# Loads of the next stage issued before both changes of stage, and the attention's product of outputs and gates moved from VectorE to POOL

## Chip, cores and metric

One core of a Trainium2 chip runs the whole program. The metric is the time of one execution in microseconds on the device. Three runs of the kernel before gave 4301.88, 4308.98 and 4311.59 us; the median is 4308.98.

## What is computed

One layer of a hybrid decoder on 2048 tokens and 16 learned meta tokens ahead of them, 1024 channels, float32. The input is RMS-normalised and projected; one branch is an RWKV-7 recurrence, the other stick-breaking attention. Each is multiplied by its own gates, projected, merged, projected again, normalised and added to the input. The change touches the attention branch and what lies on its two sides. Cut to what matters:

```python
q, k, v = heads of the projection, 16 heads of 64 channels
z = q @ k.T * 64 ** -0.5
log_keep = where(visible, log_sigmoid(-z), 0)
log_between = reverse_cumsum(log_keep) - log_keep
weights = where(visible, exp(log_sigmoid(z) + log_between), 0)
y_attention = (weights @ v) * silu(g)
```

The kernel gets `weights @ v` in another way: a reversed running product of `sigmoid(-z)` along the keys (`kept`) gives what is left of the stick, and its transpose is multiplied with the differences of neighbouring values (`dv`).

## The kernel before

`program` (L2132) runs four stages; between them stand barriers of all engines, and everything that passes from one stage to the next goes through scratch tensors in HBM.

1. **Projection**, `project_phase` (L61), called for half A and half B of the tokens. A loop over eight pairs of heads; TensorE multiplies ten blocks of weights in each (L338 to L340), the other engines make from the products what the later stages read. SyncE loads weights (L182) and stores results. In the loop POOL makes the gains, keys and steps (L824 to L844); VectorE has the running sums (a scan, L664) and splits weights into a high and a low part (a cast, L794, and a difference, L647). Semaphores of the stage are cleared by `release` (L2140) after half B, with a barrier (L2143).

2. **Attention**, `attention_phase` (L954). The work is ordered by a list that `attention_schedule` writes out. A group `g` is four tiles of 128 queries of one head; each head has four groups, and the list has 64. In a pair of heads the groups' ranks are 0, 1, 2, 3 for the even head and 3, 2, 1, 0 for the odd one; a group of rank r sees 4(r+1) tiles of keys, so the groups at the middle of a pair are the largest. For each piece of up to 512 keys TensorE makes logits in two passes (L1134 with k_high, L1135 with k_low), ScalarE takes the sigmoid (L1202), VectorE scans it backwards (L1237 for the first piece of a row, with the mask `hidden` as second input; L1240 for the others). For each tile of keys TensorE transposes `kept` (L1145), ScalarE copies that to `w` (L1212), and TensorE adds its products to `acc` (L1172), even and odd tiles of keys in separate halves of the partitions. TensorE interleaves the logits of the next group with the transposes and products of this one, and its products lag three steps behind its transposes.

   At the end of a group ScalarE copies acc's lower half (L1217), VectorE adds the halves to `total` (L1246) and multiplies that with the gates to `y` (L1250). This "sum" comes in ScalarE's and VectorE's lists four steps of values into the next group. SyncE waits for each y (`y_done`), stores it (L1072), loads the gates of group g + 2 (L1068), and then what `due_after(g)` lists: after the groups 0, 1 and 2 of a pair k_high, k_low with the steps `dv`, and `dv_diag` of the odd head, after 3, 4 and 5 queries with k_high, k_low with the steps, and dv_diag of the next even head, after 7 the queries of the next odd one. For head 0 the loads come in three parts (`FIRST_PARTS`) at the stage's start.

   POOL clears two rows of dv and the eight w (L1255, L1257) and then has one duty: as soon as dv_diag of a head has landed it loads the last partition of it, the edges (L1261, from `scr_v_edge`). TensorE waits for dv's steps and for the edges before the first product of a head (`value_steps`).

3. **RWKV**, `rwkv_programs` (L1277), a pipeline over 33 chunks of 64 tokens; SyncE first loads four constants and the first chunk's keys (KB), queries (AR) and values (VU), and TensorE begins with transposes of KB (L1421).

4. **Branches and output**, in the same block as stage 3. Nothing of them is changed.

Of the kernel before, what the change touches and what calls it, by code (L numbers as in the profile page):

```python
# [13 lines left out]
P = 128  # L14
D = 1024
# [45 lines left out]
def project_phase(nc, sem, t, io, scratch, half):  # L61
# [21 lines left out]
    with ExitStack() as ctx:  # L83
# [4 lines left out]
        up, cols = sb("up", [P, P]), sb("cols", [P, N_COLS])  # L88
        raw = [sb(f"raw{x}", [P, 1 + N]) for x in "rkv"]
        mix = [sb(f"mix{x}", [P, N]) for x in "rkv"]  # L90
        difs = [sb(f"dif{b}", [P, max(size for _, size in SG)]) for b in range(3)]
        lora = sb("lora", [P, N])
        run, rate = sb("run", [P, N]), sb("rate", [P, N])
        keep, grow = sb("keep", [P, NCG, CHUNK + 1]), sb("grow", [P, NCG, CHUNK])
        unit, gain = sb("unit", [P, N]), sb("gain", [P, N])
        ar, kb = sb("ar", [P, NCG, 2, CHUNK]), sb("kb", [P, NCG, 2, CHUNK])
# [721 lines left out]
        def _(pool):  # L818
# [34 lines left out]
            with pool.Fori(0, PAIRS) as k:  # L853
# [4 lines left out]
                for g, (at, size) in enumerate(SG):  # L858
                    value_steps(k, g, at, size)

# [6 lines left out]
def keys_of(qt):  # L867

    return META + P * (qt + 1)
# [84 lines left out]
def attention_phase(nc, sem, t, io, scratch):  # L954
# [5 lines left out]
    LAG, ZB, TB, KB, WB = 3, 2, 4, 4, 8  # L960
    FIRST_PARTS = [(0, GROUP), (GROUP, 2 * GROUP), (2 * GROUP, QT)]
    last_logits = {e[1]: e[5] for e in order if e[0] == "logits"}
    last_values = {e[1]: e[3] for e in order if e[0] == "values"}
    with ExitStack() as ctx:
        sb = lambda name, shape, dt=F32: ctx.enter_context(nc.sbuf_tensor(name, shape, dt))
        ps = lambda name, shape: ctx.enter_context(nc.psum_tensor(name, shape, F32))
        q_parts = [sb(f"q_parts{b}", [P, SEQ], F32R) for b in range(2)]
        k_high = [sb(f"k_high{b}", [P, META + SEQ], F32R) for b in range(2)]
        k_low = [sb(f"k_low{b}", [P, META + SEQ], F32R) for b in range(2)]
        dv = [sb(f"dv{b}", [P, 1 + QT, DH]) for b in range(2)]  # L970
        dv_diag = [sb(f"dv_diag{b}", [P, QT, DH]) for b in range(2)]
        longest = sum(keys_of(qt) for qt in range(QT - GROUP, QT))
        shortest = sum(keys_of(qt) for qt in range(GROUP))
        kept = [sb(f"kept{b}", [P, shortest if b >= 2 else longest]) for b in range(4)]
        keep = [sb(f"keep{b}", [P, 512]) for b in range(KB)]
        w = [sb(f"w{b}", [P, 512]) for b in range(WB)]
        low_half = sb("low_half", [DH, 512])
        total = sb("total", [DH, 512])
        gate = [sb(f"gate{b}", [DH, 512]) for b in range(2)]
        y = [sb(f"y_sb{b}", [DH, 512]) for b in range(2)]  # L980
        hidden = sb("hidden", [P, 512])
# [4 lines left out]
        const_in, cleared = sem("a_const_in"), sem("a_cleared")  # L986
        qk_first, v_first = [[sem(f"a_{x}_first{b}") for b in range(len(FIRST_PARTS))] for x in ("qk", "v")]
        edge_first, edge_in = [sem(f"a_edge_first{b}") for b in range(len(FIRST_PARTS))], [sem(f"a_edge_in{b}") for b in range(2)]
        diag_first, diag_in = [sem(f"a_diag_first{b}") for b in range(len(FIRST_PARTS))], [sem(f"a_diag_in{b}") for b in range(2)]
# [5 lines left out]
        y_sent = [sem(f"a_y_sent{b}") for b in range(2)]  # L995
# [44 lines left out]
        def _(sp):  # L1040
            def load_queries(head, first, last, done):
                u, rows, qs = head % 2, slice(DH * head, DH * head + DH), slice(P * first, P * last)
                sp.dma_start(q_parts[u][0:DH, qs].bitcast(F32), scratch["q_hi"][rows, qs]).then_inc(done, 16)
                sp.dma_start(q_parts[u][DH:P, qs].bitcast(F32), scratch["q_lo"][rows, qs]).then_inc(done, 16)

            def load_keys(head, first, last, dst, name, done):
# [3 lines left out]
                for part in (slice(0, DH), slice(DH, P)):  # L1050
                    sp.dma_start(dst[u][part, ks].bitcast(F32), scratch[name][rows, src]).then_inc(done, 16)
# [1221 lines left out]
```

## Time and profile before

| | |
|---|---|
| median of 3 runs | 4308.98 us (4301.88 to 4311.59) |
| profiled execution | 4298.37 us |
| its span, first to last instruction | 4296.6 us |
| TensorE busy | 4141.8 us (96%) |
| VectorE busy | 2380.7 us (55%) |
| ScalarE busy | 1663.7 us (39%) |
| POOL busy | 813.6 us (19%) |
| projection | up to about 2025 us |
| attention | about 2025 to 3026 us |
| mean granted clock of TensorE | 0.988 |

Engines are named PE (TensorE), PEld (its weight loads), DVE (VectorE), ACT (ScalarE), POOL and SP (SyncE; SPq is its queue). Times in the views are microseconds from the start of the span. "L1246" is a line of the kernel. In a timeline a row has its start, how long it took, engine, line, operation, out<-in, how many like it were merged into it, and in brackets how long the engine had stood idle and what ended that. A DMA's own time in a timeline is that of its issue. Ends of matmuls are modelled.

### The profile page before, as it was taken

How to read it: one execution, taken by the hardware profiler on the slowest of the kernel's cores; microseconds unless marked ns; L12 is line 12 of the kernel's file. 1: busy time of each engine (PE TensorE's matmuls, PEld its weight loads, DVE VectorE, ACT ScalarE, POOL GpSimd, SP SyncE). 2: the span in 40 equal slices, each digit the busy share in tenths (PEclk: the TensorE clock that was granted, in tenths of full speed). 3: DMA queues.
4: the chain of work that ended last, by engine and by line, in shares of the span. 5: the costliest groups of instructions: out<-in, count | busy, mean ns of one | idle time of the engine just before them, and what ended most of it. 6: DMA issues, size and time to landing. Idle time of an engine off the chain costs nothing. (4 is left out here: it accounts for less than half of the span.)

```text
span 4296.6 us, 90884 instructions
## 1 busy us (share of the span) xinstructions
PE 4141.8 (96%) x35784; PEld 3330.3 (78%) x35784; DVE 2380.7 (55%) x3103; ACT 1663.7 (39%) x3296; POOL 813.6 (19%) x655
## 2 busy tenths in 40 slices
PE   7999999997999999998999999999799999999999
PEld 7888899986788888886666666666688888878887
DVE  5344454443444444444888877778567677633222
ACT  4222222223222222222667666766344444421112
POOL 3101111112111111110000000000356666600222
PEclk9999999998999999999999999999999999999999
DMA  2333333334334333334433443442333333365553
GB/s 91 115 120 120 112 111 103 110 101 138 99 103 118 105 106 110 111 117 138 101 83 77 99 92 82 87 85 58 98 111 101 101 101 101 87 202 175 185 187 125
DMA packets 487561, 479.81 MB, mean 112 GB/s; under 512 B 261200, under 2 KB 371408, under 8 KB 481504
## 3 DMA queue, kind: packets, MB, share of 16 engines
q1 hardware_dynamic: 475168, 450.33, 37.5%
q10 hardware_dynamic: 11520, 25.17, 1.6%
q8 instruction: 221, 3.62, 0.4%
q14 instruction: 76, 0.62, 0.1%
q0 software_dynamic: 576, 0.07, 0.0%
HBM read 305.51 MB, written 169.93 MB: 111 GB/s over the span
## 5 line engine op out<-in xcount | busy, mean ns | idle before, releaser
L1240 DVE TENSOR_TENSOR_SCAN kept<-keep,kept 128x512 f32<-128x512 f32 (+1 forms) x448 | 436.6, 974 | 59.9 <-ACT keep L1202 18.4
L1202 ACT ACTIVATE keep<-z 128x512 f32<-128x512 f32 (+3 forms) x704 | 342.4, 505 | 239.2 <-PE z L1135 228.7
L1145 PE MATMUL turned<-t_identity,kept 128*128 128x128 f32 (+1 forms) x2432 | 376.6, 277 | 23.4 <-DVE kept L1240 23.4
L1212 ACT COPY w<-turned 128x512 f32<-128x512 f32 (+4 forms) x704 | 363.2, 528 | 81.4 <-PE turned L1145 80.0
L1145 PEld LDWEIGHTS turned<-t_identity,kept 128*128 128x128 f32 (+1 forms) x2432 | 277.5, 135 | 134.2 <-ACT w L1212 45.6
L1237 DVE TENSOR_TENSOR_SCAN kept<-keep,hidden 128x512 f32<-128x512 f32 (+3 forms) x256 | 284.3, 1116 | 144.1 <-ACT keep L1202 143.5
L1172 PE MATMUL acc<-w,dv 128*64 128x512 f32 (+3 forms) x1280 | 317.5, 555 | 0.0
L1134 PE MATMUL z<-k_high,q_parts 128*128 128x512 f32 (+3 forms) x704 | 300.6, 428 | 17.0 <-DMA k_low<-scr_k_lo 15.4
L1134 PEld LDWEIGHTS z<-k_high,q_parts 128*128 128x128 f32 x704 | 133.7, 190 | 167.3 <-ACT keep L1202 96.6
L1135 PE MATMUL z<-k_low,q_parts 128*128 128x512 f32 (+3 forms) x704 | 250.1, 359 | 0.0
L1675 POOL TENSOR_TENSOR off<-NT,tri 128x512 f32<-128x512 f32 x165 | 206.0, 1276 | 173.7 <-ACT NT L1579 173.7
L1510 PE MATMUL even<-T,off 64*64 64x64 f32 x5280 | 197.2, 222 | 14.6 <-DVE T L1642 3.6
L1589 ACT COPY T<-odd 128x256 f32<-128x256 f32 x264 | 98.1, 372 | 273.1 <-PE odd L1525 261.6
L1510 PEld LDWEIGHTS even<-T,off 64*64 64x64 f32 x5280 | 176.0, 135 | 32.3 <-issue 17.8
L1261 POOL DMA_DIRECT2D dv_diag<-scr_v_edge x18 | 9.1, 504 | 922.0 <-DMA dv_diag<-scr_dv 922.0
L1657 DVE STREAM_TRANSPOSE T<-T 128x256 f32<-128x256 f32 x264 | 117.4, 445 | 100.9 <-ACT T L1589 94.3
L1648 DVE TENSOR_TENSOR X<-even,eye 128x256 f32<-128x256 f32 x330 | 139.0, 421 | 41.7 <-PE even L1510 34.0
L2016 DVE TENSOR_TENSOR y_lo<-y_raw,y_hi 128x512 fp32r<-128x512 f32 x61 | 44.7, 733 | 206.3 <-ACT y_hi L1960 206.3
L1525 PE MATMUL odd<-X,T 64*64 64x64 f32 x4224 | 155.5, 222 | 2.5 <-issue 2.2
L1525 PEld LDWEIGHTS odd<-X,T 64*64 64x64 f32 x4224 | 136.5, 135 | 16.4 <-issue 2.8
L794 DVE CAST w_hi0B<-w_raw0B 128x1024 fp32r<-128x1024 f32 x40 | 41.8, 1044 | 193.4 <-PE pp3B L340 69.3
L794 DVE CAST w_hi0A<-w_raw0A 128x1024 fp32r<-128x1024 f32 x40 | 32.5, 813 | 203.3 <-PE pp4A L340 76.4
(555 smaller groups left out, 10810.1 us busy)
## 6 DMA issues: line engine op xcount, KB each, us to landing
w_raw0A<-in_w_main SPq DMA_DIRECT2D x42, 512.0 KB, 3.8
w_raw0B<-in_w_main SPq DMA_DIRECT2D x42, 512.0 KB, 3.9
w_raw1A<-in_w_main SPq DMA_DIRECT2D x41, 512.0 KB, 4.0
w_raw1B<-in_w_main SPq DMA_DIRECT2D x41, 512.0 KB, 3.9
KB<-scr_kb SPq DMA_DIRECT2D x33, 512.0 KB, 5.4
AR<-scr_ar SPq DMA_DIRECT2D x33, 512.0 KB, 5.4
y_raw<-scr_y SPq DMA_DIRECT2D x64, 256.0 KB, 4.8
merge<-scr_merge SPq DMA_DIRECT2D x64, 256.0 KB, 5.5
```

The costliest lines, as they stand in the source:

```text
L1134: pe.matmul(out, queries, k_high[u][:, k0:k0 + size], start=True, stop=False)
L1135: pe.matmul(out, queries, k_low[u][:, k0:k0 + size], start=False, stop=True).then_inc(logits_done, 1)
L1145: mm = pe.transpose(turned[num % TB][0:size, P * r:P * r + P], kept[kept_in(g)][:, src:src + size], t["identity"][:, :])
L1172: mm = pe.matmul(out, lhs, rhs, start=start, stop=stop, skip_group_check=True)
L1202: act.activation(keep[num % KB][:, 0:size], z[num % ZB][:, 0:size], ACT.Sigmoid, scale=-DH ** -0.5).then_inc(keep_done, 1)
L1212: act.copy(w[num % WB][0:size, c0:512], turned[num % TB][0:size, c0:512]).then_inc(copied, 1)
L1237: dve.tensor_tensor_scan(dst, data, hidden[:, 512 - size:][:, ::-1], 1.0, ALU.mult, ALU.max).then_inc(scanned, 1)
L1240: dve.tensor_tensor_scan(dst, data, data, kept[kept_in(g)][:, end:end + 1], ALU.mult, ALU.bypass).then_inc(scanned, 1)
L1510: mm = pe.matmul(x_bank(half)[hs, k, :], off[lv - 1][hs, HP * half + k, :], T2[hs, half, 0, k, :], start=True, stop=True)
L1525: mm = pe.matmul(p_bank(half)[hs, 0, k, :], T2[hs, half, 1, k, :], X[hs, half, k, :], start=True, stop=True)
L1648: dve.tensor_tensor(X[:, half, :, :], x_bank(half), eye[:, :].unsqueeze(1).broadcast_to([P, HP, C]), ALU.add).then_inc(s["x_out"], 1)
L1675: pool.tensor_tensor(out, a, b, op).then_inc(s[name], 1)
```

## The change

Three things are done.

- **Tiles and loads of the attention's first head move ahead of the first change of stage.** The attention's tiles are laid out in `program`, in a new order, so that those of head 0 lie over tiles that the projection no longer uses at its end (their order is changed as well). `first_head_loader` loads all of head 0's operands and `hidden`; POOL issues it at the end of half B's program, after it has waited for the last `logits_pe`, `vt_pe` and `bonus_done`. These semaphores live outside the set that `release` clears. The loads in three parts are gone; TensorE waits for whole operands.
- **Loads of the RWKV stage's first chunk and its constants move into the attention.** SyncE issues them after the store and the gates of group 59. The wait for the last stores of y moves from the end of the attention's SyncE program into SyncE's program of the next stage.
- **The product with the gates moves to POOL**, behind VectorE's sum. POOL's program becomes one loop over the 64 groups; the loads of the edges stand in it, behind the product of the group after the one whose end let dv_diag be loaded. Only two of the eight w are cleared.

```diff
+def first_head_loader(io, scratch, a, head0):
+
+    def load(pool):
+        rows = slice(0, DH)
+        pool.memset(a["dv"][0][:, 0, :], 0.0).then_inc(head0.zeroed, 1)
+        pool.dma_start(a["q_parts"][0][0:DH, :].bitcast(F32), scratch["q_hi"][rows, :]).then_inc(head0.queries, 16)
+        pool.dma_start(a["q_parts"][0][DH:P, :].bitcast(F32), scratch["q_lo"][rows, :]).then_inc(head0.queries, 16)
+        for tile, name in ((a["k_high"][0], "k_hi"), (a["k_low"][0], "k_lo")):
+            for part in (slice(0, DH), slice(DH, P)):
+                pool.dma_start(tile[part, :].bitcast(F32), scratch[name][rows, PAD:TOK]).then_inc(head0.keys, 16)
+        by_tile = scratch["dv"][CHUNK:TOK, rows].rearrange("(k p) c -> p k c", p=P)
+        pool.dma_start(a["dv_diag"][0][:, :, :], by_tile).then_inc(head0.diagonal, 16)
+        pool.wait_ge(head0.zeroed, 1)
+        pool.dma_start(a["dv"][0][0:META, 0, :], scratch["dv"][PAD:CHUNK, rows]).then_inc(head0.steps, 16)
+        pool.dma_start(a["dv"][0][:, 1:, :], by_tile).then_inc(head0.steps, 16)
+        pool.dma_start(a["hidden"][:, :], io["hidden"]).then_inc(head0.const_in, 16)
+        pool.wait_ge(head0.diagonal, 16)
+        edge = scratch["v_edge"][:, rows].rearrange("(o k) c -> o k c", o=1)
+        pool.dma_start(a["dv_diag"][0][P - 1:P, :, :], edge).then_inc(head0.edges, 16)
+
+    return load
...
@@ project_phase, end of POOL's program @@
+            if first_head is not None:
+                now(pool, logits_pe, PAIRS - 1, G - 1)
+                now(pool, vt_pe, PAIRS - 1, G - 1)
+                now(pool, bonus_done, PAIRS - 1, G - 1)
+                first_head(pool)
...
@@ attention_phase, SyncE @@
-            for p, (first, last) in enumerate(FIRST_PARTS):
-                load_queries(0, first, last, qk_first[p])
...
+            load_gate(0)
+            load_gate(1)
             for g in range(GROUPS_ALL):
                 sp.wait_ge(y_done, g + 1)
                 store_y(g)
                 if g + 2 < GROUPS_ALL:
                     load_gate(g + 2)
+                if g == GROUPS * (HEADS - 1) - 1:
+                    load_chunk(sp)
...
-            for b in range(2):
-                sp.wait_ge(y_sent[b], 16 * (GROUPS_ALL // 2))
...
@@ attention_phase, VectorE @@
                     dve.tensor_tensor(total[:, :], acc[g % 2][0:DH, :], low_half[:, :], ALU.add).then_inc(total_done, 1)
-                    dve.wait_ge(total_done, g + 1)
-                    dve.wait_ge(gate_in[g % 2], 16 * (g // 2 + 1))
-                    reach(dve, y_sent[g % 2], 16 * (g // 2))
-                    dve.tensor_tensor(y[g % 2][:, :], total[:, :], gate[g % 2][:, :], ALU.mult).then_inc(y_done, 1)
...
@@ attention_phase, POOL @@
-            for tile in dv:
-                pool.memset(tile[:, 0, :], 0.0).then_inc(cleared, 1)
-            for tile in w:
-                pool.memset(tile[:, :], 0.0).then_inc(cleared, 1)
...
-            for head in range(1, HEADS):
-                pool.wait_ge(diag_in[head % 2], 16 * ((head + 1) // 2 if head % 2 else head // 2))
-                load_edges(head, 0, QT, edge_in[head % 2])
+            pool.memset(w[0][:, :], 0.0).then_inc(cleared, 1)
+            pool.memset(w[5][:, :], 0.0).then_inc(cleared, 1)
+            pool.memset(dv[1][:, 0, :], 0.0).then_inc(cleared, 1)
+
+            for g in range(GROUPS_ALL):
+                pool.wait_ge(total_done, g + 1)
+                pool.wait_ge(gate_in[g % 2], 16 * (g // 2 + 1))
+                reach(pool, y_sent[g % 2], 16 * (g // 2))
+                pool.tensor_tensor(y[g % 2][:, :], total[:, :], gate[g % 2][:, :], ALU.mult).then_inc(y_done, 1)
+                for head, what in due_after(g - 1):
+                    if what == "diagonal":
+                        u, rows = head % 2, slice(DH * head, DH * head + DH)
+                        pool.wait_ge(diag_in[u], 16 * ((head + 1) // 2 if u else head // 2))
+                        edge = scratch["v_edge"][:, rows].rearrange("(o k) c -> o k c", o=1)
+                        pool.dma_start(dv_diag[u][P - 1:P, :, :], edge).then_inc(edge_in[u], 16)
...
@@ rwkv_programs: what SyncE issued first is now issued in the attention, by load_chunk @@
+    def load(sp):
+        sp.dma_start(r["KB"][0][:, :, :, :], chunk_keys(scratch, 0)).then_inc(opening.keys, 16)
+        sp.dma_start(r["AR"][0][:, :, :, :], chunk_queries(scratch, 0)).then_inc(opening.queries, 16)
+        v = chunk_values(scratch, 0)
+        sp.dma_start(r["VU"][0][DH:P, :, 0, :], v[:, :, 0, :]).then_inc(opening.values, 16)
+        sp.dma_start(r["VU"][0][0:DH, :, 1, :], v[:, :, 1, :]).then_inc(opening.values, 16)
+        sp.dma_start(r["tri"][:, :, :], io["tri"].rearrange("p (k c) -> p k c", c=C)).then_inc(opening.const_in, 16)
+        sp.dma_start(r["full"][0][:, :], io["full_even"]).then_inc(opening.const_in, 16)
+        sp.dma_start(r["full"][1][:, :], io["full_odd"]).then_inc(opening.const_in, 16)
+        sp.dma_start(r["eye"][:, :], io["eye2"]).then_inc(opening.const_in, 16)
...
-            load_keys(0, 0)
-            load_queries(0, 0)
-            load_values(0, 0)
+            for part_sent in y_parts_sent:
+                sp.wait_ge(part_sent, 16 * (GROUPS_ALL // 2))
```

## Rows read from the trace of the kernel before

**Rows 1.** Stages by window: busy us (x instructions) by engine, clock, DMA share, GB/s

```profile
2169.59:2214.28 44.69, 41.69 (x242) 26.91 (x241) 41.83 (x43) 31.13 (x67) 0.00 (x0) 1.00 0.48 101
2214.28:2292.02 77.74, 77.67 (x466) 47.87 (x465) 57.03 (x63) 53.68 (x119) 0.97 (x2) 1.00 0.37 79
```

**Rows 2.** VectorE's groups of instructions by line in 2169.59:2214.28

```profile
L1250 DVE TENSOR_TENSOR y_sb<-total,gate 64x512 f32<-64x512 f32 x3 | 2.1, 684 | 0.1
```

**Rows 3.** Timeline of the first change of stage

```profile
2024.96 0.23 POOL L1255 MEMSET dv<- 128x64 f32 x2 [48.06 <-POOLq L2143]
...
2031.14 0.49 PE L1134 MATMUL z<-k_high,q_parts 128*128 128x144 f32 x1 [11.34 <-DMA k_low<-scr_k_lo]
...
2038.52 0.79 PE L1134 MATMUL z<-k_high,q_parts 128*128 128x512 f32 x1 [4.07 <-DMA k_low<-scr_k_lo]
```

**Rows 4.** Timeline of the second change of stage

```profile
3021.23 0.68 DVE L1250 TENSOR_TENSOR y_sb<-total,gate 64x512 f32<-64x512 f32 x1
...
3026.26 0.36 SPq L1344 DMA_DIRECT2D tri<-in_tri  x1
...
3031.80 1.94 PE L1421 MATMUL flip<-t_identity,KB 128*128 128x128 f32 x8 [10.35 <-DMA KB<-scr_kb]
```

**Rows 5.** SyncE's waits, 2020 to 3060: us in total, times, longest

```profile
SPq L1103 <- DMA scr_y<-y_sb: 1.8, 1, 1.8
```

**Rows 6.** Windows of the projection's end and of the attention's first loads

```profile
1960.00:2020.00 60.00, 59.80 (x270) 48.83 (x269) 14.66 (x19) 10.45 (x18) 2.08 (x2) 1.00 0.51 147
...
2034.00:2038.00 4.00, 0.45 (x3) 0.35 (x2) 2.25 (x3) 0.67 (x2) 0.70 (x1) 0.50 0.79 217
```

**Rows 7.** Windows of the low clock (0.50) at both changes of stage

```profile
2023.00:2043.40 20.40, 7.83 (x24) 5.65 (x24) 6.11 (x8) 4.10 (x10) 5.20 (x12) 0.50 0.74 187
3026.40:3036.60 10.20, 4.80 (x34) 4.50 (x36) 0.48 (x1) 1.07 (x2) 0.00 (x0) 0.50 0.86 263
```

**Rows 8.** POOL's groups by line over the span

```profile
L1675 POOL TENSOR_TENSOR off<-NT,tri 128x512 f32<-128x512 f32 x165 | 206.0, 1276 | 173.7 <-ACT NT L1579 173.7
```

**Rows 9.** Timeline of VectorE and POOL in the projection; the last row alone

```profile
1929.18 1.22 DVE L664 TENSOR_TENSOR_SCAN runB<-t_restart,runB 128x512 f32<-128x512 f32 x1
...
1929.35 2.14 POOL L828 TENSOR_TENSOR gainB<-gainB,mixkB 128x512 f32<-128x512 f32 x1 [0.67 <-DVE mixkB L655]
...
1930.31 1.73 DVE L794 CAST w_hi0B<-w_raw0B 128x1024 fp32r<-128x1024 f32 x1
...
1975.19 0.69 DVE L794 CAST w_hi0B<-w_raw0B 128x1024 fp32r<-128x1024 f32 x1 [8.67 <-PE pp3B L340]
```

**Rows 10.** POOL's load of the edges (L1261): head 1's, and all 18

```profile
2099.99 0.52 POOL L1261 DMA_DIRECT2D dv_diag<-scr_v_edge  x1 [50.10 <-DMA dv_diag<-scr_dv]
...
DMA to landing us min/median/max: 1.6/1.8/5.6
```

**Rows 11.** Timeline where head 1's values begin, and head 15's

```profile
2115.20 1.08 PE L1172 MATMUL acc<-w,dv 128*64 128x512 f32 x4
2115.75 0.66 DVE L1246 TENSOR_TENSOR total<-acc,low_half 64x512 f32<-64x512 f32 x1
...
2974.88 1.08 PE L1172 MATMUL acc<-w,dv 128*64 128x512 f32 x4
...
2975.42 0.66 DVE L1246 TENSOR_TENSOR total<-acc,low_half 64x512 f32<-64x512 f32 x1
```

**Rows 12.** Timeline before head 2's values begin

```profile
2164.24 0.68 DVE L1246 TENSOR_TENSOR total<-acc,low_half 64x512 f32<-64x512 f32 x1 [0.69 <-ACT low_half L1217]
...
2169.59 1.07 PE L1172 MATMUL acc<-w,dv 128*64 128x512 f32 x4
```

**Rows 13.** TensorE's weight loads' waits from 2040; two rows of the timeline

```profile
PEld z L1134 <- DMA k_low<-scr_k_lo: 1.2, 5, 0.4
...
2699.74 0.60 PE L1145 MATMUL turned<-t_identity,kept 128*16 128x128 f32 x4 [0.95 <-DVE kept L1240]
...
2197.36 0.77 DVE L1240 TENSOR_TENSOR_SCAN kept<-keep,kept 128x272 f32<-128x272 f32 x1
```

More of the change, by code:

```diff
@@ L964, in attention_phase @@
     with ExitStack() as ctx:
-        sb = lambda name, shape, dt=F32: ctx.enter_context(nc.sbuf_tensor(name, shape, dt))
         ps = lambda name, shape: ctx.enter_context(nc.psum_tensor(name, shape, F32))
[L967 to L981, printed above, removed]
+        q_parts, k_high, k_low, dv, dv_diag = a["q_parts"], a["k_high"], a["k_low"], a["dv"], a["dv_diag"]
+        kept, keep, w, hidden = a["kept"], a["keep"], a["w"], a["hidden"]
+        low_half, total, gate, y = a["low_half"], a["total"], a["gate"], a["y"]
         z = [ps(f"z{b}", [P, 512]) for b in range(ZB)]
@@ L1040, in _, with load_queries @@
         def _(sp):
[L1041 to L1046, printed above, removed]
+            def load_queries(head, done):
@@ L1047, in load_keys @@
                 u, rows = head % 2, slice(DH * head, DH * head + DH)
-                k0 = P * first + (META if first else 0)
-                ks, src = slice(k0, P * last + META), slice(PAD + k0, PAD + P * last + META)
+                sp.dma_start(q_parts[u][0:DH, :].bitcast(F32), scratch["q_hi"][rows, :]).then_inc(done, 16)
+                sp.dma_start(q_parts[u][DH:P, :].bitcast(F32), scratch["q_lo"][rows, :]).then_inc(done, 16)
+            def load_keys(head, dst, name, done):
+                u, rows = head % 2, slice(DH * head, DH * head + DH)
@@ L1050, in load_keys, with load_steps @@
                 for part in (slice(0, DH), slice(DH, P)):
-                    sp.dma_start(dst[u][part, ks].bitcast(F32), scratch[name][rows, src]).then_inc(done, 16)
-            def load_steps(head, first, last, done):
-                u, rows, tiles = head % 2, slice(DH * head, DH * head + DH), slice(first, last)
+                    sp.dma_start(dst[u][part, :].bitcast(F32), scratch[name][rows, PAD:TOK]).then_inc(done, 16)
+            def load_steps(head, done):
+                u, rows = head % 2, slice(DH * head, DH * head + DH)
@@ L1055, in load_steps @@
                 by_tile = scratch["dv"][CHUNK:TOK, rows].rearrange("(k p) c -> p k c", p=P)
[L1056 to L1062 removed]
+                if head == 1:
+                    sp.wait_ge(cleared, 3)
```

183 lines of the change are left out of this document (104 added, 79 removed).

## Prediction

> **What bounds the kernel now.** I read the windows by stage first. In the attention stage one pair of heads (eight groups of queries) takes 122.4 us and eight such pairs make the stage. In the first three groups of a pair VectorE is the fuller engine (41.83 of 44.69 us, TensorE 41.69); in the other five TensorE is full, 77.67 of 77.74 us, and VectorE has 57.03 [rows 1]. So time taken off VectorE can pay in the first 44.7 us of a pair only, and time in which TensorE stands still in the last 77.7 us is lost. VectorE's product of outputs and gates is 3 x 0.684 us in that first stretch [rows 2].
>
> Then the timelines of the two changes of stage. At the first, TensorE starts the attention 6.2 us after the new stage's first instruction, because it waits for k_low, and stops for 4.07 us more at the second part of the loads [rows 3]. At the second, the new stage's first instruction comes at 3026.26, after SyncE has waited 1.8 us for the last y to land [rows 4, 5], and TensorE starts at 3031.80, waiting for KB [rows 4].
>
> **The preload at the first change.** POOL has nothing to do for 48.06 us ahead of the barrier [rows 3]. The new load issues 11 transfers there, and holds POOL until dv_diag has landed; nothing else is queued behind it but the barrier. They carry about 4.5 MB (two q_parts of 512 KB, four key parts of 516 KB, dv and dv_diag of 512 KB each, hidden of 256 KB, by the tiles' shapes), which over 46 us is 98 GB/s beside the 147 GB/s of that stretch [rows 6]; the start of the attention shows that 217 GB/s and more are moved when asked [rows 6]. So I cost the transfers at nothing. Bounds: nothing below, and above it the whole gain of this change of stage plus some wait at the barrier, 10 us, since no row shows POOL issue transfers of thousands of 256 B pieces. The gain: TensorE starts at about 2025.05 in place of 2031.14, 6.1 us, and the 4.07 us go too, because VectorE, which paces the stage's opening, ran dry there. **-10.1 us.** TensorE's clock was granted at its low level (1.2 GHz) from 2023 to 2043.4 after it had stood idle, and TensorE was busy for only 7.83 of those 20.4 us [rows 7]. It may rise sooner now; VectorE sets the pace there, so I take 0, bound -2.
> POOL's six memsets fewer, the new order of the tiles and the semaphores' new homes: 0; they run beside TensorE's first products, and no engine waits for POOL there now.
>
> **The preload at the second change.** Eight transfers move to SyncE's queue behind the store of group 59, where SyncE has the length of a group (122.4/8, some 15 us) until its next store; none of them is on a path. After the change the barrier no longer waits for the last y to land. But y's end comes later: the product of group 62, which VectorE began at 3021.23 [rows 4], runs on POOL from then for 1.28 us [rows 8], then VectorE's last sum (0.66) from 3022.55, then POOL's last product to 3024.5 and the store's issue (0.47) to 3025.1. With 0.5 us for the barrier (an estimate: the last store's issue ends near 3024, the wait of 1.8 us follows, and the next stage begins at 3026.26) TensorE starts at 3025.7 in place of 3031.80. **-6.1 us**, bounds -8 (the low clock of 3026.4 to 3036.6 [rows 7] is avoided) and -5. SyncE waits for y's landing inside the new stage; what is behind it still comes no later than now, since the eight transfers are gone from ahead of it.
>
> **The product on POOL.** A 128x512 product with both inputs in SBUF takes POOL 1.276 us alone [rows 8], VectorE's takes 0.684. But is POOL alone? In the projection VectorE's scan runB started at 1929.18 for 1.22 us; POOL's product gainB of the same 512 elements started at 1929.35 and took 2.14 us, so it ended 1.09 us after the scan. VectorE's next cast took 1.73 us in place of 0.69 [rows 9]. That reads as one waiting for the other. The attention's scans read two tiles in SBUF each, and VectorE is ready with one as soon as the sum ends. So the product waits for that scan (up to 1.28 us), runs 1.09 us, and holds the next scan for 1.0 us. VectorE gets rid of 0.70 us and gets 1.04 us of waiting: +0.35 us for each of three groups, about +1 us a pair. With no such lock it would be -2.1 us a pair.
> The Trainium skill (SBUF — State Buffer, "Who interferes with whom") says that a VectorE instruction with two SBUF inputs contends with a GpSimd instruction that reads SBUF, and that the one issued first blocks the other fully. By that rule the product is worth nothing to VectorE here; without it, the sum below would be some 30 us smaller. The rows on the scan agree with it.
>
> **What is late next: the edges.** POOL's queue held only the loads of the edges (dv_diag's last row), each issued as soon as dv_diag had landed, at 2099.99 for head 1 [rows 10], 15 us before use. Now each stands behind a product: for an odd head behind that of the pair's fourth group. That group's sum comes after the time at which TensorE begins the values of the next head: the sum starts at 2115.75 and lasts 0.66, TensorE's first product of head 1 is at 2115.20; for head 15 the numbers are 2975.42 and 2974.88 [rows 11], and the pattern is the same in all eight pairs. TensorE waits for the edges before that very product. So the chain is: sum ends 2116.41, scan until 2117.69, product until 2118.78, issue to landing 1.8 us (the median of 18 [rows 10]) with 0.1 us of latency, 2120.65. TensorE stands for 5.4 us, in the stretch in which it is the full engine. 8 x 5.4 = **+43 us**. Bounds: 4.3 each with no lock (product alone 1.28), and 3.5 if the other engines' emptied queues give TensorE an odd microsecond back; 6 at the top. For even heads the edges stand behind the seventh group's product: its sum starts at 2164.24, TensorE needs them at 2169.59 [rows 12], the chain ends about 2168.5: 0.
>
> **k_low.** SyncE loads k_low of an odd head once y of the pair's second group is done. TensorE already waits for it in five of eight pairs, 1.2 us in all [rows 13], and soon after it stands another 0.95 us for the scans [rows 13]. y comes 1.2 us later (a 272-element scan of 0.77 [rows 13], then 1.1, less 0.7); most is covered by that wait. With VectorE's +1 us a pair I take **+8 us** for both, bounds -16 and +14.
>
> **Sum.** -10.1 - 6.1 + 43 + 8 = +35 us. The profiled execution took 4298.4 us (span 4296.6), 10.6 us under the median of the three runs, 4308.98; against itself the sum gives 4333, against the median, with which the new time will be compared, 4344.
>
> **The rivals.**
> Slower (the forecast), 0.67: as above, +20 to +50.
> Preload too late, 0.08: POOL is still making up the small pieces of dv and dv_diag when the barrier comes. All as forecast but for the -10: +45, 4354. For it: no row prices such an issue. Against it: 46 us of room.
> No lock, 0.15: the product runs beside the scans. -16.2 - 16 + 8 x 4.3 = +2 us, 4311: no difference. Against it: the scan runB and gainB.
> Faster, 0.10: TensorE's stretch at 99.9% is not its real peak (its ends are modelled, and it waits for ScalarE's copies in short pieces), so that after each stop it finds full buffers and regains 3 us of it. With the lock absent too: -16.2 - 16 + 8 x (4.3 - 3) = -22, 4287. This decides from the point at which a stop costs under some 3 us a pair. Against it: no row shows TensorE faster in such a stretch than its 77.7 us.
> That the change doesn't do what it says has no case of its own: each transfer stands in a queue ahead of its barrier.
>
> **How the numbers follow.** A measurement tells 0.2%, 8.6 us, from no change. Slower than that: the forecast and the late preload, 0.75, and the slower part of the no-lock case, 0.02; the same 0.13; faster 0.10. The range reaches from the no-lock case's better half, 4304, to the late preload with its upper bounds, 4360; the 0.10 of the faster case and the ends beyond make up what is left out.
>
> **What would show it.** TensorE's first attention matmul within 0.3 us of that stage's first instruction and no wait for k_low there; the same for KB at the second change. In the waits, TensorE waiting for the DMA dv_diag<-scr_v_edge eight times, some 40 us in total. POOL's 64 products at a mean of about 2 us, and scans after them of about 2.3 us. If the wait for the edges is missing, or POOL's product takes 1.28 us beside a scan, I am wrong on the main term or on the lock; if POOL is the last at the first barrier, on the preload.

## The result, and the profile after

| | before | after |
|---|---|---|
| median of 4 runs each | 4308.6 us (4301.88 to 4311.59) | 4375.11 us (4374.6 to 4378.25) |
| ratio after/before, 95% interval | | 1.0156 (1.0141 to 1.017) |
| profiled execution | 4298.37 us | 4375.37 us |
| mean granted clock of TensorE | 0.988 | 0.980 |

The change makes the kernel 66.5 us slower. The forecast was 4344 us (4304 to 4360): the sign was right, the loss was almost twice the +35 us forecast, and the time lies above the range.

Busy times of the engines, from the first part of the page of the kernel after:

```profile
PE 4172.5 (95%) x35784; PEld 3349.0 (77%) x35784; DVE 2378.2 (54%) x3039; ACT 1665.5 (38%) x3296; POOL 960.9 (22%) x721
```

VectorE has got rid of 64 products of 0.684 us and is only 2.5 us less busy. Most of what it gained went into longer scans, below. TensorE has the same matmuls and is 30.7 us busier: part of them ran at the lower clock.

TensorE's waits in the kernel after (us in total, times, longest):

```profile
PE acc L1203 <- DMA dv_diag<-scr_v_edge: 43.2, 8, 5.5
PE turned L1176 <- DVE kept L1271: 20.1, 9, 2.7
PE z L1165 <- DMA k_low<-scr_k_lo: 15.8, 8, 2.8
...
PE flip L1488 <- DVE S L1736: 5.5, 1, 5.5
...
PE z L1165 <- PEq L2210: 5.4, 1, 5.4
```

PEq is TensorE's sequencer; its wait here is the barrier. The first row is the late edges: eight stops. The last two are the changes of stage, both shortened. The third is new in this size: the loads of k_low, which before cost 1.2 us in five pairs [rows 13].

**The edges.** The stop in the second pair of heads, kernel after; the rows to set beside it are [rows 10, 11]:

```profile
2241.11 0.66 DVE L1277 TENSOR_TENSOR total<-acc,low_half 64x512 f32<-64x512 f32 x1
...
2241.70 1.27 DVE L1271 TENSOR_TENSOR_SCAN kept<-keep,kept 128x512 f32<-128x512 f32 x1
2241.85 2.17 POOL L1289 TENSOR_TENSOR y_sb<-total,gate 64x512 f32<-64x512 f32 x1 [21.22 <-DVE total L1277]
2243.97 0.55 POOL L1295 DMA_DIRECT2D dv_diag<-scr_v_edge  x1
...
2246.03 1.98 PE L1203 MATMUL acc<-w,dv 128*64 128x512 f32 x4 [5.38 <-DMA dv_diag<-scr_v_edge]
```

The chain is the forecast one: sum, a scan that holds POOL's product, product, issue, landing. But the four products behind the stop take 1.98 us in place of 1.08 [rows 11]. The same stretch by windows (columns as in [rows 1]), first the second pair's two stages, then the 12 us behind the stop:

```profile
2169.63:2217.16 47.53, 43.20 (x241) 28.03 (x240) 42.56 (x41) 31.09 (x67) 8.10 (x3) 0.96 0.45 95
2217.16:2302.62 85.46, 80.00 (x466) 49.19 (x465) 56.07 (x57) 53.89 (x119) 11.26 (x7) 0.96 0.34 72
...
2246.00:2252.00 6.00, 5.97 (x20) 3.16 (x20) 1.65 (x2) 2.17 (x4) 0.00 (x0) 0.60 1.01 227
2252.00:2258.00 6.00, 6.00 (x34) 3.58 (x33) 3.88 (x4) 3.56 (x7) 0.00 (x0) 1.00 0.70 147
```

Against [rows 1] the first stage of this pair is 2.8 us longer, the second 7.7 us, of which the stop is 5.4. In the 6 us behind the stop TensorE is busy and gets only 20 matmuls done, at a mean granted clock of 0.60; in the next 6 us 34, at full clock. So after this stop, in which TensorE did nothing, its clock is granted at the low level (1.2 GHz), and the stop is paid for a second time. In two stretches, the stop's last 2 us and what comes behind it:

```profile
2244.00:2246.00 2.00, 0.00 (x0) 0.00 (x1) 0.00 (x0) 0.00 (x0) 0.51 (x2) 0.50 0.29 71
2246.03:2250.70 4.67, 4.67 (x15) 2.76 (x16) 0.78 (x1) 1.19 (x3) 0.00 (x0) 0.50 1.02 232
```

The low level began within the stop and lasted 6.8 us, of which 4.7 us lie behind it. At half the clock these 4.7 us do the work of 2.3 us. By the starts of each group's first product, averaged over the six inner pairs (the second to the seventh), a pair takes 133.61 us against 122.88:

| group of the pair | 0 | 1 | 2 | 3 | 4 | 5 to 7 |
|---|---|---|---|---|---|---|
| before, us | 9.54 | 15.37 | 20.22 | 23.35 | 21.65 | 32.73 |
| after, us | 9.58 | 17.17 | 21.44 | 28.88 | 23.85 | 32.71 |

Groups 1 and 2 lose 3.0 us, the stop's group 5.5 us, the group behind it 2.2 us.

**The lock and k_low.** ("The lock" is the waiting of POOL's product and VectorE's scans for each other.) The sum of group 1 of the same pair, kernel after:

```profile
2197.96 0.66 DVE L1277 TENSOR_TENSOR total<-acc,low_half 64x512 f32<-64x512 f32 x1
...
2198.55 0.77 DVE L1271 TENSOR_TENSOR_SCAN kept<-keep,kept 128x272 f32<-128x272 f32 x1
2198.70 2.81 POOL L1289 TENSOR_TENSOR y_sb<-total,gate 64x512 f32<-64x512 f32 x1 [13.04 <-DVE total L1277]
2199.24 1.19 DVE L1268 TENSOR_TENSOR_SCAN kept<-keep,hidden 128x512 f32<-128x512 f32 x1
...
2200.53 4.60 DVE L1271 TENSOR_TENSOR_SCAN kept<-keep,kept 128x512 f32<-128x512 f32 x3
2201.53 0.47 SPq L1111 DMA_DIRECT2D scr_y<-y_sb  x1
...
2202.68 1.24 SPq L1090 DMA_DIRECT2D k_low<-scr_k_lo  x2
...
2210.65 0.50 PE L1165 MATMUL z<-k_high,q_parts 128*128 128x512 f32 x1 [1.75 <-DMA k_low<-scr_k_lo]
```

POOL's product starts 0.15 us after the scan of 272 elements and ends 1.08 us after the end of the next one, at 2200.43. It waited for two scans, where I had counted one. So k_low is issued 33.0 us after the pair's first product; before it was 29.0 us (2198.61 after 2169.59), and TensorE stops for it. VectorE's side, its scans over the whole span, after:

```profile
L1271 DVE TENSOR_TENSOR_SCAN kept<-keep,kept 128x512 f32<-128x512 f32 x240 | 330.8, 1378 | 43.4 <-ACT keep L1233 22.9 <-DVE kept L1271 0.5
L1268 DVE TENSOR_TENSOR_SCAN kept<-keep,hidden 128x512 f32<-128x512 f32 x208 | 263.9, 1269 | 116.1 <-ACT keep L1233 115.9
```

and POOL's product:

```profile
L1289 POOL TENSOR_TENSOR y_sb<-total,gate 64x512 f32<-64x512 f32 x64 | 144.5, 2257 | 920.5 <-DVE total L1277 920.5
```

Before, these scans took 1283 ns and 1209 ns; they are 22.9 and 12.4 us longer in total. The 64 products that VectorE gave away were 43.8 us.

The lock reaches TensorE by another way too. After group 0's product TensorE stood 1.81 us for a scan in this pair before the change; after it (timeline of TensorE, then the windows of the 3.3 us behind this stop, and behind the one for k_low at 2210.65):

```profile
2188.54 0.60 PE L1176 MATMUL turned<-t_identity,kept 128*16 128x128 f32 x4 [2.53 <-DVE kept L1271]
```

```profile
2189.40:2192.70 3.30, 3.30 (x16) 2.35 (x16) 2.99 (x4) 1.72 (x4) 0.00 (x0) 0.50 1.05 230
...
2210.70:2214.00 3.30, 3.30 (x23) 2.36 (x23) 1.91 (x3) 2.50 (x5) 0.00 (x0) 1.00 0.35 55
```

Behind 2.53 us the clock was at its low level, behind 1.75 us it was not. But the length of a stop this short doesn't settle it. In the kernel after, the clock fell behind all seven stops of 2.50 to 2.69 us for VectorE's scans; in e1 below, behind two of seven such stops; in the kernel before, behind two of seven of 1.8 us, for 3.4 us each. One of those two, with the windows behind it and behind the stop of 1.81 us in the second pair:

```profile
2555.05 0.78 PE L1145 MATMUL turned<-t_identity,kept 128*16 128x128 f32 x4 [1.81 <-DVE kept L1240]
...
2555.40:2558.60 3.20, 3.20 (x17) 2.59 (x15) 2.99 (x3) 1.94 (x4) 0.00 (x0) 0.50 0.58 124
2187.80:2191.00 3.20, 3.20 (x24) 2.50 (x25) 2.99 (x3) 1.74 (x5) 0.00 (x0) 1.00 0.71 155
```

What decides between the two cases is open here.

**The first change of stage**, kernel after, beside [rows 3]:

```profile
1978.30 0.73 POOL L994 DMA_DIRECT2D q_parts<-scr_q_hi  x1
...
1981.55 1.23 POOL L1000 DMA_DIRECT2D dv_diag<-scr_dv  x1
...
1984.53 0.56 POOL L1004 DMA_DIRECT2D hidden<-in_hidden  x1
...
2026.36 0.52 POOL L1281 MEMSET w<- 128x512 f32 x1 [26.11 <-POOLq L2210]
...
2026.55 0.46 PE L1165 MATMUL z<-k_high,q_parts 128*128 128x144 f32 x1 [5.36 <-PEq L2210]
```

POOL had issued all but the edges within 7 us, issued these at 1999.73, once dv_diag had landed, and stood idle for the last 26 us before the barrier. TensorE starts 0.2 us behind the stage's first instruction, and the stop for the second part is gone.

**The second change of stage**, kernel after, beside [rows 4]:

```profile
3097.79 2.59 SPq L1111 DMA_DIRECT2D scr_y<-y_sb  x2
3097.86 0.68 DVE L1277 TENSOR_TENSOR total<-acc,low_half 64x512 f32<-64x512 f32 x1 [1.44 <-POOL y_sb L1289]
3098.63 1.25 POOL L1289 TENSOR_TENSOR y_sb<-total,gate 64x512 f32<-64x512 f32 x1 [0.87 <-DVE total L1277]
...
3101.61 0.48 DVE L1736 MEMSET S<- 128x512 f32 x1 [3.07 <-PEq L1021]
3102.20 1.09 PE L1488 MATMUL flip<-t_identity,KB 128*128 128x128 f32 x4 [5.53 <-DVE S L1736]
```

The wait for KB is gone. VectorE's last sum stood 1.44 us for POOL's product of the group before, since both use `total`; what ends last is POOL's last product (3099.88) and the issue of its store (3100.38). The new stage's first instruction follows 1.23 us later, and TensorE 0.59 us behind it, since it waits for VectorE's memset of S.

The two profiled executions differ by 77.0 us, and this adds up from times read off both traces (end of the projection's last matmul, first matmul of the attention, its last product, first transpose of KB):

| part | us |
|---|---|
| end of the projection | +1.4 |
| first change of stage (11.34 to 5.36) | -6.0 |
| attention, first to last matmul (990.3 to 1070.1) | +79.8 |
| second change of stage (10.35 to 5.53) | -4.8 |
| all behind it (1264.8 to 1271.4) | +6.6 |

The 1.4 us stand before the preload begins and appear in several of the kernels below too. The 6.6 us come back under "why".

### The profile page after: what moved, and what is told of

Read it like the earlier page. It is cut to its first block and busy times, and to the rows that moved or that the text cites. A ratio compares the mean times of both kernels' runs of the same rounds, so it can differ in the third digit from the quotient of the medians.

```text
span 4373.6 us, 90861 instructions
## 1 busy us (share of the span) xinstructions
PE 4172.5 (95%) x35784; PEld 3349.0 (77%) x35784; DVE 2378.2 (54%) x3039; ACT 1665.5 (38%) x3296; POOL 960.9 (22%) x721
## 5 line engine op out<-in xcount | busy, mean ns | idle before, releaser
L1271 DVE TENSOR_TENSOR_SCAN kept<-keep,kept 128x512 f32<-128x512 f32 (+1 forms) x448 | 463.6, 1035 | 120.3 <-ACT keep L1233 81.8
L1243 ACT COPY w<-turned 128x512 f32<-128x512 f32 (+4 forms) x704 | 362.9, 528 | 81.2 <-PE turned L1176 79.8
L1268 DVE TENSOR_TENSOR_SCAN kept<-keep,hidden 128x512 f32<-128x512 f32 (+3 forms) x256 | 296.7, 1165 | 160.1 <-ACT keep L1233 159.8
L1203 PE MATMUL acc<-w,dv 128*64 128x512 f32 (+3 forms) x1280 | 327.8, 570 | 43.3 <-DMA dv_diag<-scr_v_edge 43.2
L1289 POOL TENSOR_TENSOR y_sb<-total,gate 64x512 f32<-64x512 f32 x64 | 144.5, 2257 | 920.5 <-DVE total L1277 920.5
L1165 PE MATMUL z<-k_high,q_parts 128*128 128x512 f32 (+3 forms) x704 | 306.3, 436 | 23.1 <-DMA k_low<-scr_k_lo 15.8
```

What stands on the lines that cost most here:

```text
L1165: pe.matmul(out, queries, k_high[u][:, k0:k0 + size], start=True, stop=False)
L1203: mm = pe.matmul(out, lhs, rhs, start=start, stop=stop, skip_group_check=True)
L1243: act.copy(w[num % WB][0:size, c0:512], turned[num % TB][0:size, c0:512]).then_inc(copied, 1)
L1268: dve.tensor_tensor_scan(dst, data, hidden[:, 512 - size:][:, ::-1], 1.0, ALU.mult, ALU.max).then_inc(scanned, 1)
L1271: dve.tensor_tensor_scan(dst, data, data, kept[kept_in(g)][:, end:end + 1], ALU.mult, ALU.bypass).then_inc(scanned, 1)
L1289: pool.tensor_tensor(y[g % 2][:, :], total[:, :], gate[g % 2][:, :], ALU.mult).then_inc(y_done, 1)
```

## The experiments

All were run beside the kernel before, whose medians were 4300.46 us (e1 to e4), 4300.51 us (e5 to e8) and 4301.41 us (e9 to e11), on three chips, so ratios are what is compared; 0.001 is 4.3 us. The difference of two ratios is uncertain by 0.0013 to 0.0022, that is 6 to 9 us, so small differences between experiments rest on the traces. "Group n" is a group of a pair as in the table above.

**e1, the edges first.** POOL issues the edges before it waits for the sum.

```diff
-                pool.wait_ge(total_done, g + 1)
-                ...
-                pool.tensor_tensor(y[g % 2][:, :], total[:, :], gate[g % 2][:, :], ALU.mult).then_inc(y_done, 1)
                 for head, what in due_after(g - 1):
                     ...
+                pool.wait_ge(total_done, g + 1)
+                ...
+                pool.tensor_tensor(y[g % 2][:, :], total[:, :], gate[g % 2][:, :], ALU.mult).then_inc(y_done, 1)
```

> POOL loads the edges before it waits for the group's sum; all else as in the changed kernel. Theory A (the late edges are the main loss, and TensorE's clock falls after each stop): the eight waits for dv_diag<-scr_v_edge (43 us) and the slow stretch behind them (2.2 us in each pair's fifth group) both go, a pair of heads takes 133.6 - 5.5 - 2.2 = 125.9 us, the kernel about 4313 us. Rival B (POOL's product beside the scans is the main loss, the waits for the edges overlap with it): a pair stays above 129 us, the kernel above 4335.

Measured: 4304.04 us, ratio 1.0008 (0.9999 to 1.0017). The order of two instructions in POOL's queue makes 0.0148, 64 us, of difference to the change as made. A pair takes 125.08 us, somewhat less than the 125.9 of theory A. No wait for the edges is left, groups 3 and 4 are back at 23.41 and 21.68 us. Between the two traces the attention is 68.2 us shorter (1001.9 us): eight stops of 5.4 us are 43 us, the low clock behind them 17.6 us (2.2 us in each group 4), and group 1 takes 1.1 us a pair less (16.11), where the clock now falls behind two of seven stops only. The wait for k_low stays:

```profile
PE z L1165 <- DMA k_low<-scr_k_lo: 15.4, 8, 2.6
```

**e2, the edges in the middle.** As e1, but behind the wait for the sum, ahead of the product.

> POOL loads the edges behind the wait for the sum but ahead of its product. The stop of TensorE should shrink from 5.5 to about 3.1 us (sum's end, 0.1, landing 1.8). If the clock falls after a stop of that length too, a pair costs 3.1 + 2.2 more than with the edges first: 131.2 us, kernel about 4355. If the clock holds, 129.0 us and about 4338.

Measured: 4357.71 us, ratio 1.0135 (1.0119 to 1.015). Stops:

```profile
PE acc L1203 <- DMA dv_diag<-scr_v_edge: 27.7, 8, 3.5
```

The stops are 2.0 us shorter, but group 4 still takes 24.04 us, 2.4 more than before: the low clock comes behind each of the stops of 3.45 us too. A pair takes 131.97 us, near the 131.2 expected for that case. The product of 2.2 us is only the smaller part of what made the edges late; waiting for the sum at all is the larger.

**e3, the product on VectorE.** As before the change; POOL loads the edges at once. Both preloads stay.

```diff
                     dve.tensor_tensor(total[:, :], acc[g % 2][0:DH, :], low_half[:, :], ALU.add).then_inc(total_done, 1)
+                    dve.wait_ge(total_done, g + 1)
+                    ...
+                    dve.tensor_tensor(y[g % 2][:, :], total[:, :], gate[g % 2][:, :], ALU.mult).then_inc(y_done, 1)
```

> Product back on VectorE, edges as soon as dv_diag has landed; both preloads stay. Theory A: the attention's pairs return to 122.9 us, the first change of stage keeps its gain of 8, the second its gain at the start: 4291 to 4303 us, faster than the kernel before. Rival C (the preloads cost something of their own, in the projection by their transfers or later in the RWKV stage): 4305 to 4312.

Measured: 4282.33 us, ratio 0.9959 (0.9946 to 0.9973), 17.6 us faster than before, and faster than either expectation. The forecast for the two preloads was -16.2. A pair takes 122.97 us, as before (122.88). This is the version to keep.

**e4, SyncE's loads behind the sum.** As e1, but SyncE issues what is due for the next head once `total_done` is there, and stores y behind it.

```diff
-                sp.wait_ge(y_done, g + 1)
-                store_y(g)
-                ...
+                sp.wait_ge(total_done, g + 1)
                 for head, what in due_after(g):
                     ...
+                sp.wait_ge(y_done, g + 1)
+                store_y(g)
+                ...
```

> Edges first, and SyncE issues the next head's loads behind total_done in place of y_done, product still on POOL. If the rest of the loss (3 us a pair in its second and third groups) comes from the late y that delays k_low, a pair falls from 125.9 to 123.5 us or less, 4294 us. If it comes from POOL's product holding up VectorE's scans, it stays within 0.7 us of 125.9, 4308 to 4313.

Measured: 4293.23 us, ratio 0.9983 (0.9974 to 0.9992). TensorE's waits for k_low are gone, and the pair is 1.4 us shorter than in e1 (123.65 against 125.08). That is nearly the 123.5 us expected if k_low is the cause. So of the 0.0049 (21 us) by which e1 is slower than e3, about half (0.0025, 11 us, with 6 us of uncertainty) is k_low; the other half is put down to the lock on VectorE's scans and the later end of the last group.

**e5 and e6, a shadow on POOL.** e3 with one more instruction on POOL after each sum, into a tile that nobody reads: in e5 a product of two inputs in SBUF, in e6 a memset.

```diff
+                pool.wait_ge(total_done, g + 1)
+                reach(pool, shadowed, g)
+                pool.tensor_tensor(a["shadow"][:, :], hidden[0:DH, :], hidden[0:DH, :], ALU.mult).then_inc(shadowed, 1)   # e5
+                pool.memset(a["shadow"][:, :], 0.0).then_inc(shadowed, 1)                                                # e6
```

> As e3 (product on VectorE, which sets when y comes), and POOL multiplies after each sum two SBUF tiles into a tile that nobody reads: y and all loads keep their times, only POOL's use of SBUF is added. Theory A (a two-input scan of VectorE and a POOL instruction that reads SBUF wait for each other): POOL's instruction takes some 2.0 us or more in place of 1.28, the two kinds of 512-element scans gain together 25 to 40 us over 308 + 251 us, and a pair takes 124.5 to 125.5 us against 123.0 of e3 (VectorE now has the product and the wait). Rival D (no lock; what e4 lost against e3 was POOL's later product alone): scans stay at 1283 and 1209 ns, a pair at 123.0.

> As e5, but POOL's extra instruction is a memset of that tile: it writes SBUF and reads nothing. Theory A: no waiting on either side, memset 0.53 us, scans at 1283 and 1209 ns, a pair at 123.0 us. If any POOL access to SBUF blocked the scans, they would gain some 15 us in all and the memset would take over 1 us.

Measured: e5 4308.46 us, ratio 1.0018 (1.0008 to 1.0027); e6 4283.29 us, ratio 0.9963 (0.995 to 0.9976), the same as e3. Groups by line of e5, VectorE's scans and POOL's shadow:

```profile
L1273 DVE TENSOR_TENSOR_SCAN kept<-keep,kept 128x512 f32<-128x512 f32 x240 | 324.3, 1351 | 31.1 <-ACT keep L1235 8.9 <-DVE kept L1273 0.5
...
L1300 POOL TENSOR_TENSOR shadow<-hidden 64x512 f32<-64x512 f32 x64 | 163.4, 2553 | 768.9 <-DVE total L1279 768.7
```

and of e6:

```profile
L1273 DVE TENSOR_TENSOR_SCAN kept<-keep,kept 128x512 f32<-128x512 f32 x240 | 307.8, 1283 | 35.0 <-ACT keep L1235 13.7 <-DVE kept L1273 0.5
...
L1300 POOL MEMSET shadow<- 64x512 f32 x64 | 33.2, 519 | 850.5 <-DVE total L1279 850.5
```

A product on POOL that no instruction waits for costs 25 us (0.0059) by itself; a write on POOL with no read costs nothing that can be told, and the scans keep their 1283 ns. The cost reaches TensorE in two ways: its waits for the scans grow from 23.1 us in e3 to 35.9 us, and the clock falls behind the stop in group 1 in seven of the eight pairs, where it fell in two in e3. A pair takes 125.85 us, a little above the expected 124.5 to 125.5. The Trainium skill (SBUF — State Buffer, "Who interferes with whom") says that VectorE with two SBUF inputs contends with a GpSimd instruction that reads SBUF, not with one that only writes it; both runs agree.

**e7 and e8, each preload taken away.** e3 without the first preload (the three-part loads of before, by SyncE), and e3 with the chunk loads issued in the new stage.

```diff
-            project_phase(nc, sem, t, io, scratch, HALF_B, first_head_loader(io, scratch, a, head0))      # e7
+            project_phase(nc, sem, t, io, scratch, HALF_B)
...
-                if g == GROUPS * (HEADS - 1) - 1:      # e8
-                    load_chunk(sp)
...
+            opening_loader(io, scratch, r, opening)(sp)
```

> As e3 without the preload at the first change: head 0 is loaded in three parts by SyncE at the stage's start, as before the change. TensorE's first attention matmul to its last is 3 to 4 us longer than in e3 (the second part's wait) and the first comes 6 us later after the projection's end: 9 us over e3, ratio to before 0.9975 to 0.9985.

> As e3 without the preload at the second change (constants and chunk 0 loaded first thing in the RWKV stage; the barrier still does not wait for y). TensorE's last attention matmul to its first transpose of KB: 3.96 us in e3, 8 to 10 us here. If the RWKV stage keeps a head start, the kernel is 4 to 6 us slower than e3; if it gives it back (as the changed kernel's RWKV stage seemed to, whose end came 1.8 us later after the last attention matmul than before), within 1.5 us of e3.

Measured: e7 4291.99 us, ratio 0.9981 (0.9972 to 0.999); e8 4290.14 us, ratio 0.9981 (0.9971 to 0.9991). Against e3 each preload is worth 0.0022, 9.5 us, with 7 us of uncertainty. For e7 that is what was expected; for e8 it is more than the 4 to 6 us. The timeline of e7 shows the two stops of before again:

```profile
2031.19 0.49 PE L1184 MATMUL z<-k_high,q_parts 128*128 128x144 f32 x1 [11.65 <-DMA k_low<-scr_k_lo]
...
2038.32 0.79 PE L1184 MATMUL z<-k_high,q_parts 128*128 128x512 f32 x1 [3.83 <-DMA k_low<-scr_k_lo]
```

In e8 TensorE starts after 12.35 us and waits for `eye`, the last of the loads in this order, where it was 10.35 us and KB before. By these 2 us e8 overstates its preload.

**e9, only the edges late.** e3 with the edges behind VectorE's product; POOL computes nothing.

```diff
+                pool.wait_ge(y_done, g + 1)
                 for head, what in due_after(g - 1):
```

> Both preloads, the product on VectorE, no product on POOL anywhere; only the edges are late: POOL issues them once VectorE's product of the group is done. TensorE should stop eight times for about 3.8 us (sum 0.66 + product 0.69 + issue to landing 1.9 + the 0.55 by which its first product stands ahead of the sum). Theory (a stop is paid for twice, once as idle time and once at the low clock in the group behind it, 2.2 us each): 4282 + 8 x 6.0 = 4330, with the group of the stop 3.8 us and the next group 2.2 us longer. Rival (the 2.2 us belong to POOL's product and its hold on VectorE's scans): 4282 + 8 x 3.8 = 4312, next group unchanged at 21.68 us.

Measured: 4346.68 us, ratio 1.011 (1.0095 to 1.0126); against e3 +0.0151, 65 us (58 us between the profiled executions). Its waits and its second pair's last five groups (columns as in [rows 1]):

```profile
PE acc L1203 <- DMA dv_diag<-scr_v_edge: 43.5, 8, 5.9
```

```profile
2212.09:2296.99 84.90, 79.56 (x465) 48.86 (x464) 57.14 (x63) 53.77 (x119) 0.97 (x2) 0.96 0.34 72
```

The stop was 5.4 us, not the 3.8 expected, so the total of either theory (4330 and 4312) was too low; group by group the theory holds. Group 3 took 28.83 us, group 4 23.75 us, 2.1 us more than in e3, with no product on POOL at all. The loss in the group behind the stop belongs to the stop. Why the stop was longer shows here:

```profile
2106.92 0.68 DVE L1281 TENSOR_TENSOR y_sb<-total,gate 64x512 f32<-64x512 f32 x1
...
2107.63 0.47 SPq L1111 DMA_DIRECT2D scr_y<-y_sb  x1
...
2108.29 0.49 POOL L1296 DMA_DIRECT2D dv_diag<-scr_v_edge  x1 [82.18 <-DVE y_sb L1281]
...
2111.28 1.97 PE L1203 MATMUL acc<-w,dv 128*64 128x512 f32 x4 [5.53 <-DMA dv_diag<-scr_v_edge]
```

SyncE issued 0.03 us after the product's end, POOL 0.69 us after it, and TensorE went on 2.99 us after that issue began; in the kernel after it was 2.06 us. In e9 the transfer stood behind SyncE's store and gates, issued from 0.66 us earlier on; in the second pair of the kernel after POOL issued at 2243.97, just ahead of SyncE's store at 2244.04. That this made the landing later fits both traces and wasn't tried by itself; why POOL began 0.69 us late is open.

**e10, the loads behind the sum with VectorE's product.** e4's edit to SyncE's queue, on e3.

> The version with the product on VectorE and both preloads, and SyncE's loads of the next head issued once the sum is done, ahead of y's store, rather than 0.7 us later once y is done. Theory (TensorE waits for k_low in some pairs, 1.2 us in all, before VectorE's scans): gone, but nearly all of it is given back to the scans' wait that ends last next: 4281, no difference that can be told from 4282. Rival (k_low is the last wait there): 4274.

Measured: 4283.07 us, ratio 0.9964 (0.995 to 0.9978): no difference to e3. With the product on VectorE the 0.7 us by which y follows the sum holds nothing up.

**e11, the product alone.** The changed kernel with e7's and e8's edits: no preloads.

> The changed kernel without its two preloads: the first head's loads in three parts and the chunks' first loads at their stages, the product on POOL with the edges behind it. Theory (preloads and product add up; each preload was worth 8 us beside VectorE's product): 4375 + 16 = 4391. Rival (the preloads lose their worth beside POOL's product, as the trace of the changed kernel's last stage suggests for the second): 4380 to 4384.

Measured: 4385.94 us, ratio 1.0196 (1.018 to 1.0212), 84 us slower than before. With both preloads it is 1.0156: by the ratios they are worth 0.0040, 17 us with 9 us of uncertainty, beside POOL's product (0.0041 beside VectorE's). That doesn't decide between the theory and the rival: the time lies between 4384 and 4391, and the medians of e11 and of the kernel after are 10.8 us apart, the profiled executions 12.0. At the changes of stage themselves the traces show the whole worth. TensorE's first attention matmul comes 11.84 us after the projection's end, not 5.36, and its first product 15.02 us behind that, not 12.16 (9.3 us together); the second change takes 14.06 us, not 5.53 (8.5 us, of which some 2 are, as in e8, the wait for `eye`). But in e11 the rest of the attention is 3.7 us shorter and all behind the second change 2.5 us shorter, with no cause shown.

## Why the prediction was right in sign and wrong in size

The change falls into two parts. Both preloads: -17.6 us (e3). The product with what hangs on it: +84 us (e11). Together +66.7, measured +66.5. Each part is uncertain by 6 to 7 us, and the measured change by 6 us, so that they meet this closely is luck; that they add up within some 10 us is what is shown.

- **The first preload**: forecast -10.1. The trace after shows -6.0 to the first matmul, and from there the first product comes 3.5 us earlier (12.16 in place of 15.66 us): -9.5. e7 gives 9.5 us. POOL was done 26 us before the barrier, so the case of the late preload is false. TensorE's low clock behind the barrier lasted 10.2 us in place of the 20.4 of [rows 7]. TensorE was busy for 9.35 of these 10.2 us and VectorE for 7.59, so that VectorE sets the pace there isn't what this trace shows; but the sum of the term, with 0 for the clock, came out right.
- **The second preload**: forecast -6.1. With VectorE's product the start of the stage gains 6.4 us (10.35 to 3.96 in e3), with POOL's 4.8. The forecast chain from the start of group 62's product to the end of the last product was right: 3.3 us forecast, 3.37 measured (3096.51 to 3099.88). What failed by 1.3 us is what stands behind it: the 0.5 us for the barrier, which took 1.23 us from the end of the last store's issue to the stage's first instruction (0.82 us in e3), and VectorE's memset of S, which the forecast left out and for which TensorE's first transpose comes 0.59 us after that instruction, not within 0.3. The stretch from the first transpose to the end took 1271.4 us in the profile after, against 1264.8 before; in the profiles of the eleven experiments it lay between 1263.7 and 1268.9. I have no cause for that spread, and it stays open. Whether the preload kept its worth to the end of the kernel beside POOL's product, e11 leaves open.
- **The edges**: forecast 8 x 5.4 = +43; measured 43.2, by the chain as it was told, and e1 takes them away. Right.
- **The clock behind the stops**: this is the first step that failed. I priced the low clock at the changes of stage and not behind the eight new stops, though the sum had TensorE standing for 5.4 us each time. It costs 2.2 us a pair, 17.6 us in all, so a stop costs 7.6 us in place of 5.4. e9 shows it with no product on POOL, e2 shows it for stops of 3.45 us.
- **k_low and VectorE's scans**: the second step that failed: "y comes 1.2 us later; most is covered by that wait", +8. e1 against e3 gives 0.0049, 21 us: about half for k_low (e4), half for the scans. The mechanism was right, the size was not. The product of group 1 waited for two scans, and y followed the sum's end by 2.9 us rather than the 0.7 of before; the sum itself came 1.9 us later in its pair; and I took the wait of 1.2 us in five pairs for slack that would cover the rest, where it was the sign of a load with none. And the stop for the scans behind group 0 grew from 1.81 to 2.53 us, with 3.4 us of low clock behind it in seven pairs; the forecast had neither. With the edges first the stops were as long and the clock fell in two pairs only (e1), some 8 us less; what decides it is open.
- **No lock** (0.15): false, by e5 and e6. POOL's products took 2.26 us on average, as forecast, and the 45 scans of 512 keys that stood behind one took 2.03 us on average, 2.33 at most (forecast about 2.3). **Faster** (0.10): false; group 3 takes the whole stop (+5.5), and TensorE regains nothing.

The forecast of +51 for the product, with 17.6 for the clock and 13 more for k_low and the scans, is +82; e11 measured +84, with 7 us of uncertainty, and the 8 us of the low clock in group 1 lie within that. The range's top was worked out from terms that all left the clock out.

## What to carry to other kernels

A stop of TensorE of a few us inside a full stretch costs more than its length: add what the low clock takes from the matmuls behind it, read from the rows of the same kernel at either level (here 2.2 us behind each 5.4 us, and about the same behind 3.45 us). Behind stops of 1.8 to 2.7 us the clock fell in some runs and held in others, so there give a range.

Before work goes to an idle engine's queue, list what that queue already holds and when each item is needed: a DMA of 0.5 us that stood behind a product cost 64 us, and moving it ahead took one edit. A product moved from VectorE to POOL gained nothing here, since VectorE's next instructions read two tiles in SBUF: it waits for them and they wait for it. And a small wait for a load (1.2 us in five places) says that the load has no slack left.

Preloading through an idle queue ahead of a barrier brought what the timeline of before promised (16.2 forecast, 17.6 measured).

## What the runs showed of the hardware

- In the kernel after TensorE's granted clock was 0.50 for 6.8 us at each of the eight stops of 5.4 us, from about 2 us before the stop's end, and for 3.4 us behind each of the seven stops of 2.50 to 2.69 us for VectorE's scans. Stops as short can go either way: in e1 it fell behind two of seven of 2.50 to 2.69 us, in the kernel before behind two of seven of 1.8 us. The mean granted clock of the run (0.980 against 0.988) hardly shows them.
- POOL's product could wait for two scans of VectorE in a row (2.81 us, of which 1.08 us lie behind the second scan's end). Over all 64 products its length went from 1.25 to 3.07 us, with a median of 2.18.
- POOL issued a transfer of thousands of 256 B pieces in 1.23 and 1.29 us, little more than twice the 0.55 us of a load with long rows; the landing of `dv_diag` took 17.9 us beside the others, and nobody waited for it but POOL.
